# Results of seven experts by way of a table in device memory, in a two-layer decoder trunk

## The chip, the cores and the metric

The kernel runs on one core of a Trainium2 chip. The metric is the device time of one execution in microseconds (us), lower being better; where several runs are given, it is their median. A profiled execution gives a span (first to last instruction of the program) and a trace of every instruction and transfer.

The engines are called TensorE (PE in the rows), VectorE (DVE), ScalarE (ACT), GpSimd (POOL) and SyncE (SP). SBUF is the on-chip memory, PSUM the memory that TensorE's products go to (tile PS, eight banks of 128x512).

## What is computed

Two layers, each with three token mixers and a channel mixer, for 256 tokens of 1024 channels in float32. The second layer's channel mixer, the last thing before the output, picks two of eight experts per token:

```python
def swiglu(h, w1, w3, w2):
    return (jax.nn.silu(h @ w1) * (h @ w3)) @ w2

def moe_swiglu(h, w_router, w1, w3, w2):
    logits = (h @ w_router).astype(jnp.float32)
    top_val, top_idx = lax.top_k(logits, TOP_K)          # TOP_K = 2
    probs = jax.nn.softmax(top_val, axis=-1)
    combine = jnp.sum(jax.nn.one_hot(top_idx, N_EXPERTS, dtype=jnp.float32) * probs[..., None], axis=-2)
    out = jnp.zeros_like(h)
    for e in range(N_EXPERTS):                            # 8 experts, inner width 3584
        out = out + combine[..., e:e + 1] * swiglu(h, w1[e], w3[e], w2[e])
    return out
```

The layer's result is `x + moe_swiglu(h, ...)`. The mixers, norms and the dense channel mixer of the first layer are untouched by the change.

## The kernel before

**Arithmetic.** Every product of float32 matrices is made of three: each operand is split into a high part (hi, rounded to the format that TensorE multiplies fast) and a residue (lo), and `products` (lines 476 to 478) adds hi x hi, hi x lo and lo x hi in PSUM.

**Weight units.** SyncE loads weights in units of 1 MB, in a fixed order, into six slots `raw`. ScalarE copies each unit to one of three slots `hi` (line 1186); VectorE subtracts that copy from the raw unit, which gives `lo`, in the raw slot's own place (line 1681). Both call this step `prep`. TensorE counts a unit as used (`unit_used`) after its last product with it. The load of unit u waits for unit u-6 to be used, ScalarE's copy for unit u-3. Each engine works through its own list in order, so a `prep` stands between other operations at a place written out by hand.

**Experts.** There are 128 slots for the tokens of an expert. Per expert there are seven steps (`step`, inner width 512 each): `up` for w1 and w3 (four units, into PS banks 0 and 1), SiLU by ScalarE (f_s), the product by VectorE (f_g), four transposes (`turn_f`, line 1063), the split into fT_hi (ScalarE) and fT_lo (VectorE), and `down` for w2 (two units, summed in banks 4 and 5). Banks 4 and 5 hold the expert's result, one row per slot, after its last `down`, which TensorE runs inside the next expert's first step. If more than 128 tokens chose one expert, the flag `r_flag` starts a second round of all experts (`turn` 1) for the rest; in the measured data it doesn't run.

**Which tokens.** `r_t[:, 14]` holds for each token and expert the token's slot. VectorE makes the 0/1 matrix `pick` (token by slot, `choose`); `find_rows` multiplies it by token numbers, VectorE turns that into indices (`keep_row`), and GpSimd fetches the tokens' rows from `fn_dram` by an indirect transfer into `e_rows` (line 2455), half an expert ahead. `turn_rows` transposes them for the next expert.

**Adding results, before.** In the next expert ScalarE copies banks 4 and 5 to y_hi and VectorE makes y_lo (`results`). TensorE turns `pick` (two transposes, line 1099), ScalarE copies that to `pickT`, and `scatter` (line 1026) multiplies it by y_hi and y_lo: eight matmuls of 128x512 put each slot's row back at its token, in banks 4 to 7. VectorE adds that to `x` with the token's weight for the expert, `r_t[:, 15]` (`add_to_x`, line 2235, two operations). For the last expert `scatter_last` and `add_last` do it in halves, and SyncE stores `x`.

GpSimd has nothing else to do in the experts than the gathers of rows.

## Time and profile before

| | us |
|---|---|
| median of 3 runs | 2058.24 |
| lowest and highest run | 2054.41, 2058.87 |
| profiled execution | 2054.22 |
| its span | 2052.4 |

| engine | busy us | share of the span |
|---|---|---|
| TensorE (PE) | 2012.1 | 98% |
| VectorE (DVE) | 1580.0 | 77% |
| ScalarE (ACT) | 1247.0 | 61% |
| GpSimd (POOL) | 13.9 | 1% |

The experts take the second half, from about 1077 us on. Of the 516.53 MB that were moved, 336 units of 1 MB are expert weights, and in that half the rate is 329 to 382 GB/s per slice of the page, against 80 to 277 GB/s in the first half. A matmul's duration in the trace includes the time it takes to run through the array; matmuls overlap, so their pace is read from how far apart they start. Idle time of an engine that isn't the bottleneck costs nothing.

### The profile page before, as it was taken

Reading aid. Unit: us, or ns where it says so; the run is one execution under the profiler, and the core shown is the slowest. Engines: PE = TensorE matmul, PEld = TensorE weight load, DVE = VectorE, ACT = ScalarE, POOL = GpSimd, SP = SyncE. Lnnn points to the kernel's source line nnn. Section 1 sums busy time; section 2 is a strip of 40 time slices with the busy share of each in tenths; the row PEclk is TensorE's granted clock in tenths of the full one; section 3 lists DMA queues with packets and bytes.
Section 4 is the critical chain, followed back from the end, with each engine's and each line's share of the span. In section 5 each row is a group of like instructions: output and inputs, shape, how many; then the busy total and the mean of one; then the engine's idle time right before and its main releaser. Section 6 shows DMA issues by size and latency. Waiting matters only on the chain.

```text
span 2052.4 us, 28693 instructions
## 1 busy us (share of the span) xinstructions
PE 2012.1 (98%) x10737; PEld 1722.1 (84%) x10737; DVE 1580.0 (77%) x1218; ACT 1247.0 (61%) x1060; POOL 13.9 (1%) x21
## 2 busy tenths in 40 slices
PE   9999999999999999999989999999999999999998
PEld 8988888789998987888878888888888888888887
DVE  5778855755445878865768898888989889898987
ACT  5655455443334664455447777777777777777775
POOL 0000000000000000000000000000000000000000
PEclk9999999999999999999999999999999999999999
DMA  8523455255554523455249999999999999999996
GB/s 277 167 80 106 143 182 184 83 184 185 184 184 146 183 83 103 144 172 182 98 154 329 378 364 380 370 358 377 358 382 353 380 369 357 377 358 381 354 374 243
DMA packets 240765, 516.53 MB, mean 252 GB/s; under 512 B 11528, under 2 KB 34312, under 8 KB 240686
## 3 DMA queue, kind: packets, MB, share of 16 engines
q1 hardware_dynamic: 238274, 507.33, 69.9%
q0 software_dynamic: 2144, 7.88, 1.1%
q8 instruction: 55, 0.90, 0.2%
q10 hardware_dynamic: 268, 0.22, 0.0%
q14 instruction: 24, 0.20, 0.0%
HBM read 513.28 MB, written 2.12 MB: 251 GB/s over the span
## 4 chain that ended last, share of the span: by engine, by line
PE 92%; DVE 4%; issue 2%; ACT 2%; DVEq 0%; ACTq 0%
PE PS L476 27%; PE PS L478 27%; PE PS L477 27%; PE PS L560 7%; PE PS L1063 1%; ACT hi L1186 1%; PE PS L1026 1%; PE PS L780 1%; PE PS L694 0%; PE PS L811 0%; DVE t_n L1704 0%; PE PS L1014 0%; DVE b_gc L2014 0%; PE PS L493 0%; PE PS L649 0%
## 5 line engine op out<-in xcount | busy, mean ns | idle before, releaser
L1681 DVE TENSOR_TENSOR lo<-raw,hi 128x2048 fp32r<-128x2048 f32 x481 | 1095.8, 2290 | 289.9 <-ACT hi L1186 287.6
L1186 ACT ACTIVATE hi<-raw 128x2048 fp32r<-128x2048 f32 x481 | 919.7, 1915 | 314.1 <-PE PS L478 307.9
L476 PE MATMUL PS<-hi,e_hi 128*128 128x512 f32 x896 | 355.1, 396 | 1.4 <-DVE e_lo L1704 1.4
L478 PE MATMUL PS<-hi,e_lo 128*128 128x512 f32 x896 | 349.5, 390 | 0.0
L477 PE MATMUL PS<-lo,e_hi 128*128 128x512 f32 x896 | 349.0, 389 | 0.0
L476 PE MATMUL PS<-hi,actT_hi 128*128 128x512 f32 x640 | 253.4, 396 | 3.7 <-DVE lo L1681 3.1
L478 PE MATMUL PS<-hi,actT_lo 128*128 128x512 f32 x640 | 249.6, 390 | 0.0
L477 PE MATMUL PS<-lo,actT_hi 128*128 128x512 f32 x640 | 249.2, 389 | 0.0
L476 PE MATMUL PS<-hi,fT_hi 128*128 128x512 f32 x536 | 208.7, 389 | 0.0
L478 PE MATMUL PS<-hi,fT_lo 128*128 128x512 f32 x536 | 208.7, 389 | 0.0
L477 PE MATMUL PS<-lo,fT_hi 128*128 128x512 f32 x536 | 208.6, 389 | 0.0
L478 PEld LDWEIGHTS PS<-hi,e_lo 128*128 128x128 f32 x896 | 168.2, 188 | 36.1
L476 PEld LDWEIGHTS PS<-hi,e_hi 128*128 128x128 f32 x896 | 168.3, 188 | 34.6 <-DVE e_lo L1704 1.6
L477 PEld LDWEIGHTS PS<-lo,e_hi 128*128 128x128 f32 x896 | 168.5, 188 | 33.3
L476 PE MATMUL PS<-actT_hi,hi 128*128 128x256 f32 x672 | 191.4, 285 | 1.4 <-DVE actT_lo L1704 1.4
L478 PE MATMUL PS<-actT_hi,lo 128*128 128x256 f32 x672 | 190.7, 284 | 0.0
L477 PE MATMUL PS<-actT_lo,hi 128*128 128x256 f32 x672 | 190.7, 284 | 0.0
L476 PEld LDWEIGHTS PS<-hi,actT_hi 128*128 128x128 f32 x640 | 120.3, 188 | 28.2 <-ACT hi L1186 3.9
L478 PEld LDWEIGHTS PS<-hi,actT_lo 128*128 128x128 f32 x640 | 120.1, 188 | 25.4
L477 PEld LDWEIGHTS PS<-lo,actT_hi 128*128 128x128 f32 x640 | 120.3, 188 | 23.6
L476 PEld LDWEIGHTS PS<-actT_hi,hi 128*128 128x128 f32 x672 | 129.5, 193 | 2.3 <-issue 1.8
L477 PEld LDWEIGHTS PS<-actT_lo,hi 128*128 128x128 f32 x672 | 129.6, 193 | 0.4
(329 smaller groups left out, 2112.0 us busy)
## 6 DMA issues: line engine op xcount, KB each, us to landing
raw<-in_moe_w SPq DMA_DIRECT2D x336, 1024.0 KB, 5.3
raw<-in_w_in SPq DMA_DIRECT2D x92, 1024.0 KB, 5.1
raw<-in_ffn_w SPq DMA_DIRECT2D x33, 1024.0 KB, 5.2
raw<-in_w_br SPq DMA_DIRECT2D x12, 1024.0 KB, 5.0
raw<-in_w_out SPq DMA_DIRECT2D x8, 1024.0 KB, 5.1
bias<-hankel_dram POOLq DMA_DIRECT2D x1, 1536.0 KB, 12.7
x<-in_x SPq DMA_DIRECT2D x2, 512.0 KB, 5.5
f_gain<-in_norm_ffn POOLq DMA_DIRECT2D x2, 512.0 KB, 3.8
```

The source lines that it names most:

```text
L476: pe.matmul(out, a_hi, b_hi, start=first, stop=False, skip_group_check=True)
L477: pe.matmul(out, a_hi, b_lo, start=False, stop=False, skip_group_check=True)
L478: return pe.matmul(out, a_lo, b_hi, start=False, stop=last, skip_group_check=True)
L560: return pe.matmul(out, a, b, start=first, stop=last)
L780: ins = pe.transpose(PS[:, 4 + h // 2, ((h % 2) * TT + t) * P:((h % 2) * TT + t + 1) * P], c_n[:, t, hs(h)], ident)
L1026: ins = pe.matmul(PS[:, 4 + 2 * t + half, :], pickT[:, t, :], src[:, half * 512:(half + 1) * 512], start=part == 0, stop=part == 1)
L1063: ins = pe.transpose(PS[:, 2, j * P:(j + 1) * P], f_g[0][:, j * P:(j + 1) * P], ident)
L1186: act.activation(hi[prog.u % SPLIT][:, :], raw[slot][:, :], COPY).then_inc(hi_made.sem, 1)
L1681: dve.tensor_tensor(lo[prog.u % RAW][:, :], raw[prog.u % RAW][:, :], hi[s][:, :].bitcast(F32), ALU.subtract).then_inc(lo_made.sem, 1)
```

## The change

For `turn` 0, which is all that runs on the measured data, the first seven experts' results no longer pass through TensorE.

- ScalarE copies banks 4 and 5 to a float32 tile `y_out` (`results_out`) in the place of y_hi, at the same point of its list. GpSimd writes it to a table `y_dram` in device memory, 128 rows of 4 KB per expert (0.52 MB).
- The scatter, the transposes of `pick`, the copy to `pickT`, y_lo and `add_to_x` are gone in these experts. The last expert keeps `scatter_last` and `add_last`, with its own transposes.
- VectorE computes in the first expert, for each token and each of its two choices, the row of the table (`places`, seven small operations): the slot plus 128 times the expert's number. A token whose choice is the last expert (or lies past slot 128) gets a row of the table's last 128, which hold zeros; GpSimd writes these at the start.
- In the last expert GpSimd waits for the seventh write, starts four indirect transfers into `y_back` (two choices by two halves of the tokens, 0.52 MB each), multiplies each by the token's weight and adds it to `x`: eight operations on 128x1024 with both inputs in SBUF. `add_last` waits for them (`y_added`).

```diff
+        def results_out(n, used):
+            act.wait_ge(unit_used.sem, used)
+            act.wait_ge(fn_out.sem, n * 16 + 32)
+            act.activation(y_out[:, :], bank(4, 5), COPY).then_inc(y_hi_made.sem, 1)
...
             up(0)
-            if not first:
+            if turn and not first:
                 scatter(n - 1)
-            for t in range(TT):
-                ins = pe.transpose(PS[:, 3, t * P:(t + 1) * P], pick[:, t, :], ident)
-            ins.then_inc(pickT_done.sem, 1)
+            if turn or last:
+                for t in range(TT):
+                    ins = pe.transpose(PS[:, 3, t * P:(t + 1) * P], pick[:, t, :], ident)
+                ins.then_inc(pickT_done.sem, 1)
             up(1)
-            if not first:
-                pe.wait_ge(s_read.sem, s_read.count(2 * n - 1))
+            if turn and not first:
+                pe.wait_ge(s_read.sem, s_read.count((n - SPREAD) * 2 - 1))
+            elif not first:
+                pe.wait_ge(y_hi_made.sem, n)
             down(base, first=True)
...
         def add_last(n, e, turn):
+            dve.wait_ge(y_added.sem, 2 * TT)
...
+        def places():
+            dve.wait_ge(slots_here.sem, 6)
+            pos, base, val, part = (r_t[:, n, :] for n in (14, 16, 17, 18))
+            tt(val, pos, base, ALU.add).then_inc(dve_step.sem, 1)
+            dve.wait_ge(dve_step.sem, prog.step())
+            dve.scalar_tensor_tensor(val, pos, float(P), val, ALU.is_lt, ALU.mult).then_inc(dve_step.sem, 1)
+            dve.wait_ge(dve_step.sem, prog.step())
+            for k in range(2):
+                tt(part, r_t[:, 4 + k, :], val, ALU.mult).then_inc(dve_step.sem, 1)
+                dve.wait_ge(dve_step.sem, prog.step())
+                dve.tensor_reduce(r_t[:, 19, k * TT:(k + 1) * TT], part.rearrange("p (t e) -> p t e", t=TT),
+                                  AX.X, ALU.add).then_inc(dve_step.sem, 1)
+                dve.wait_ge(dve_step.sem, prog.step())
+            dve.tensor_scalar(y_at[:, :], r_t[:, 19, 0:2 * TT], float(SPREAD * P), None, ALU.add).then_inc(row_made.sem, 1)
...
             prep(2)
             multiply(base + 1, U + 8)
             prep(2)
+            if first and turn == 0:
+                places()
             if not last:
                 choose(n + 1, e + 1, turn)
             low(base + 1)
...
         for n in range(1, E):
-            pool.wait_ge(row_made.sem, n)
+            pool.wait_ge(row_made.sem, n + 1)
             if n > 1:
                 pool.wait_ge(e_done.sem, e_done.count(2 * n))
             pool.indirect_dma_start(e_rows[:, :], None, fn_dram[:, :],
                                     bass.IndirectOffsetOnAxis(ap=row_i[:, 0:1], axis=0)).then_inc(e_rows_here.sem, 16)
+            pool.wait_ge(y_hi_made.sem, n)
+            pool.dma_start(y_dram[(n - 1) * P:n * P, :], y_out[:, :]).then_inc(fn_out.sem, 16)
+        pool.wait_ge(fn_out.sem, 32 + 16 * SPREAD)
+        for c in range(2 * TT):
+            pool.indirect_dma_start(y_back[:, c, :], None, y_dram[:, :],
+                                    bass.IndirectOffsetOnAxis(ap=y_at[:, c:c + 1], axis=0)).then_inc(e_rows_here.sem, 16)
+        pool.wait_ge(e_rows_here.sem, 16 * (SPREAD + 2 * TT))
+        for c in range(2 * TT):
+            t = c % TT
+            pool.tensor_tensor(y_back[:, c, :], y_back[:, c, :], r_t[:, 11, c:c + 1].broadcast_to([P, D]), ALU.mult)\
+                .then_inc(y_scaled.sem, 1)
+            pool.wait_ge(y_scaled.sem, c + 1)
+            if c >= TT:
+                pool.wait_ge(y_added.sem, c - TT + 1)
+            pool.tensor_tensor(x[:, t, :], x[:, t, :], y_back[:, c, :], ALU.add).then_inc(y_added.sem, 1)
```

What this does to the lists. TensorE at the boundary from the first expert to the second, between the two halves of the second step's `up`, before (the numbers at the ends of names tell buffers apart):

```order
L478 MATMUL PS<-hi_61,e_lo_153 128x512
L1022 REGISTER_ALU
L1026 MATMUL PS<-y_hi,pickT 128x512
L1026 MATMUL PS<-y_lo,pickT 128x512
L1026 MATMUL PS<-y_hi,pickT 128x512
L1026 MATMUL PS<-y_lo,pickT 128x512
L1026 MATMUL PS<-y_hi,pickT 128x512
L1026 MATMUL PS<-y_lo,pickT 128x512
L1026 MATMUL PS<-y_hi,pickT 128x512
L1026 MATMUL PS<-y_lo,pickT 128x512
L1099 MATMUL PS<-consts,pick 128x128 x2
L476 MATMUL PS<-hi_62,e_hi_151 128x512
```

and now:

```order
L485 MATMUL PS<-hi_61,e_lo_153 128x512
L489 REGISTER_ALU
L483 MATMUL PS<-hi_62,e_hi_151 128x512
L484 MATMUL PS<-lo_56,e_hi_151 128x512
L485 MATMUL PS<-hi_62,e_lo_153 128x512
```

The eight matmuls of the scatter and the two transposes are gone, and the products of the next half of `up` follow those of the first.

VectorE in the first expert, second step, now, with the seven operations of `places` between two residues (`lo`), the pick and fT_lo:

```order
L1699 TENSOR_TENSOR lo_55<-raw_49,hi_61 128x2048
L1722 TENSOR_TENSOR r_t<-r_t 128x16
L2277 SCALAR_TENSOR_TENSOR r_t<-r_t 128x16
L1722 TENSOR_TENSOR r_t<-r_t 128x16
L2282 TENSOR_REDUCE r_t<-r_t 128x2
L1722 TENSOR_TENSOR r_t<-r_t 128x16
L2282 TENSOR_REDUCE r_t<-r_t 128x2
L2285 TENSOR_SCALAR y_at<-r_t 128x4
L2234 TENSOR_SCALAR pick<-slots,r_t 128x128 x2
L1722 TENSOR_TENSOR fT_lo_139<-PS,fT_hi_137 128x512
L1699 TENSOR_TENSOR lo_56<-raw_50,hi_62 128x2048
```

Before, the pick followed the residue `lo_55` at once.

GpSimd's list from the last gather of rows to its end, now:

```order
L2501 DMA e_rows<-fn_dram,row_i 128x1024
L2504 DMA y_dram<-y_out 128x1024
L2507 DMA y_back<-y_dram,y_at 128x1024 x4
L2512 TENSOR_TENSOR y_back<-y_back,r_t 128x1024
L2517 TENSOR_TENSOR x<-x,y_back 128x1024
L2512 TENSOR_TENSOR y_back<-y_back,r_t 128x1024
L2517 TENSOR_TENSOR x<-x,y_back 128x1024
L2512 TENSOR_TENSOR y_back<-y_back,r_t 128x1024
L2517 TENSOR_TENSOR x<-x,y_back 128x1024
L2512 TENSOR_TENSOR y_back<-y_back,r_t 128x1024
L2517 TENSOR_TENSOR x<-x,y_back 128x1024
```

Before, its list ended with the seventh gather of rows; the write of a result now follows each of the seven.

## Rows read from the trace of the kernel before

**Rows 1.** Busy time per engine in a stretch of the experts, with its heading.

```profile
core 0: us, PE busy (x) PEld busy (x) DVE busy (x) ACT busy (x) POOL busy (x), PEclk, DMA share, GB/s
1320.00:1440.00 120.00, 120.00 (x551) 99.46 (x550) 107.28 (x65) 88.39 (x60) 0.95 (x1) 1.00 1.00 368
```

**Rows 2.** Waits from 1065 us on: who for whom, us in total, times, longest.

```profile
ACT hi L1186 <- PE PS L478: 137.5, 213, 3.9
...
PE PS L476 <- DVE e_lo L1704: 1.4, 1, 1.4
```

**Rows 3.** Order in time, last expert: start us, us, engine, line, tiles, idle before.

```profile
1965.17 1.92 ACT L1186 ACTIVATE hi<-raw 128x2048 fp32r<-128x2048 f32 x1 [0.80 <-PE PS L478]
1967.89 1.92 ACT L1186 ACTIVATE hi<-raw 128x2048 fp32r<-128x2048 f32 x1 [0.80 <-PE PS L478]
...
1967.26 2.28 DVE L1681 TENSOR_TENSOR lo<-raw,hi 128x2048 fp32r<-128x2048 f32 x1
```

**Rows 4.** Groups from 1050 us on: busy us, mean ns of one, idle before.

```profile
L1681 DVE TENSOR_TENSOR lo<-raw,hi 128x2048 fp32r<-128x2048 f32 x336 | 764.8, 2289 | 105.5 <-ACT hi L1186 104.7
...
L1704 DVE TENSOR_TENSOR f_g<-f_s,PS 128x512 f32<-128x512 f32 x56 | 38.1, 680 | 0.1
...
L2235 DVE SCALAR_TENSOR_TENSOR x<-PS,r_t,x 128x1024 f32<-128x1024 f32 x14 | 17.3, 1276 | 0.0
...
L1704 DVE TENSOR_TENSOR y_lo<-PS,y_hi 128x1024 fp32r<-128x1024 f32 x7 | 8.5, 1218 | 0.0
```

**Rows 5.** Tile raw (1200 to 2040 us); transfers (1371 to 1378 us); one stretch; issues.

```profile
L1681 DVE TENSOR_TENSOR lo<-raw,hi x292: 2277/2292/2295, 1200.1 to 2038.0; 128x2048 fp32r<-128x2048 f32 x146
...
DMA to landing us min/median/max: 4.8/5.3/7.9
...
q0 software_dynamic: 144, 0.52, 19.6%
...
1380.00:1390.00 10.00, 10.00 (x48) 8.26 (x47) 8.86 (x5) 7.51 (x6) 0.00 (x0) 1.00 1.04 399
...
raw<-in_moe_w SPq DMA_DIRECT2D x336, 1024.0 KB, 5.3
```

**Rows 6.** TensorE in time at the last boundary.

```profile
1940.36 0.40 PE L478 MATMUL PS<-hi,e_lo 128*128 128x512 f32 x1
1940.59 0.40 PE L1026 MATMUL PS<-y_hi,pickT 128*128 128x512 f32 x1
...
1942.46 0.38 PE L1099 MATMUL PS<-consts,pick 128*128 128x128 f32 x2
1942.59 0.47 PE L476 MATMUL PS<-hi,e_hi 128*128 128x512 f32 x1
1942.91 0.39 PE L477 MATMUL PS<-lo,e_hi 128*128 128x512 f32 x1
```

**Rows 7.** VectorE in time at the same boundary.

```profile
1938.22 4.50 DVE L1681 TENSOR_TENSOR lo<-raw,hi 128x2048 fp32r<-128x2048 f32 x2
```

**Rows 8.** VectorE in time: small operations of the routing, a residue of the first expert.

```profile
1063.99 0.17 DVE L2372 SCALAR_TENSOR_TENSOR r_t<-r_t 128x16 f32<-128x16 f32 x1
1064.20 0.17 DVE L2361 TENSOR_REDUCE r_t<-r_t 128x2 f32<-128x16 f32 x1
...
1109.12 4.59 DVE L1681 TENSOR_TENSOR lo<-raw,hi 128x2048 fp32r<-128x2048 f32 x2 [0.30 <-ACT hi L1186]
```

**Rows 9.** GpSimd in time.

```profile
1059.78 0.39 POOL L2443 CAST slots<-slots_i 128x256 f32<-128x256 int32 x1
...
1060.43 0.18 POOL L2447 CAST ids<-slots_i 128x2 f32<-128x2 int32 x1
...
1129.11 2.70 POOL L2455 DMA_INDIRECT e_rows<-fn_dram,row_i  x1 [60.99 <-DVE row_i L2221]
1249.64 0.96 POOL L2455 DMA_INDIRECT e_rows<-fn_dram,row_i  x1 [117.83 <-DVE row_i L2221]
1370.72 0.95 POOL L2455 DMA_INDIRECT e_rows<-fn_dram,row_i  x1 [120.12 <-DVE row_i L2221]
```

More of the change, by code:

```diff
@@ L68 @@
 PAIRS = E // 2
+SPREAD = E - 1
 K_ID, K_LE, K_GT, K_M0, K_MT, K_N = 0, 1, 2, 3, 4, 11
@@ L1019, in scatter @@
         def scatter(n):
-            pe.wait_ge(pickT_made.sem, n + 1)
-            pe.wait_ge(y_lo_made.sem, y_lo_made.count(n + 1))
+            pe.wait_ge(pickT_made.sem, n - SPREAD + 1)
+            pe.wait_ge(y_lo_made.sem, y_lo_made.count(n - SPREAD + 1))
             for t in range(TT):
@@ L1030, in scatter_last @@
         def scatter_last(n, turn):
-            pe.wait_ge(pickT_made.sem, n + 1)
+            pe.wait_ge(pickT_made.sem, n - SPREAD + 1)
             for half in range(2):
                 if half:
-                    pe.wait_ge(y_lo_made.sem, y_lo_made.count(n + 1))
+                    pe.wait_ge(y_lo_made.sem, y_lo_made.count(n - SPREAD + 1))
                 else:
@@ L1113, in expert @@
             if not last:
-                if not first:
-                    pe.wait_ge(s_read.sem, s_read.count(2 * n))
+                if turn and not first:
+                    pe.wait_ge(s_read.sem, s_read.count((n - SPREAD) * 2))
                 if turn == 0:
@@ L1133, in experts @@
             if turn:
-                pe.wait_ge(s_read.sem, s_read.count(2 * E * turn))
+                pe.wait_ge(s_read.sem, s_read.count(2))
             n = E * turn
@@ L1599, in expert @@
             prep(2 if first else 4)
-            if not first:
+            if not first and turn:
                 results(U + 4)
+            elif not first:
+                results_out(n - 1, U + 4)
             high(base)
@@ L1606, in expert @@
             prep(1)
-            act.wait_ge(pickT_done.sem, pickT_done.count(n + 1))
-            act.activation(flat(pickT), PS[:, 3, 0:T], COPY).then_inc(pickT_made.sem, 1)
+            if turn or last:
+                act.wait_ge(pickT_done.sem, pickT_done.count(n - SPREAD + 1))
+                act.activation(flat(pickT), PS[:, 3, 0:T], COPY).then_inc(pickT_made.sem, 1)
             prep(3)
@@ L2211, in choose @@
             dve.wait_ge(e_done.sem, e_done.count(2 * n))
-            dve.wait_ge(pickT_done.sem, pickT_done.count(n))
+            if turn:
+                dve.wait_ge(pickT_done.sem, pickT_done.count(n - SPREAD))
             for t in range(TT):
@@ L2278, in expert @@
             prep(1 if first else 2)
-            if not first:
+            if turn and not first:
                 results(n - 1)
@@ L2283, in expert @@
             prep(1)
-            if not first:
+            if turn and not first:
                 for t in range(TT):
@@ L2409, in moe @@
                 prep(3)
-                dve.wait_ge(s_read.sem, s_read.count(2 * E))
+                dve.wait_ge(s_read.sem, s_read.count(2))
                 experts(1)
@@ L2447, in _ @@
         pool.tensor_copy(ids[:, :], slots_i[:, 0:TT]).then_inc(slots_here.sem, 1)
+        pool.wait_ge(slots_here.sem, 4)
+        pool.iota(slots_i[:, 0:TT * E], pattern=[[0, TT], [P, E]], base=-SPREAD * P, channel_multiplier=0)\
+            .then_inc(slots_here.sem, 1)
+        pool.wait_ge(slots_here.sem, 5)
+        pool.tensor_copy(r_t[:, 16, :], slots_i[:, 0:TT * E]).then_inc(slots_here.sem, 1)
+        pool.memset(y_out[:, :], 0.0).then_inc(slots_here.sem, 1)
         pool.wait_ge(norm_made.sem, norm_made.at(1, 5))
@@ L2577, in store @@
             load(out[:, :, 0:512], x[:, :, 0:512], out_here)
-            sp.wait_ge(s_read.sem, s_read.count(2 * E * (turn + 1)))
+            sp.wait_ge(s_read.sem, s_read.count(2 + 2 * E * turn))
             load(out[:, :, 512:D], x[:, :, 512:D], out_here)
```

13 lines of the change are left out of this document (10 added, 3 removed).

## Prediction, made before the changed kernel was run

> **What bounds the kernel now.** I read the profile in this order: the busy time by stretch, the waits, the order in time at an expert's boundary, then the transfers. From about 1077 us to 2043 us the eight experts run. TensorE is busy for all 120.00 us of a 120 us stretch there, at a granted clock of 1.00, and VectorE for 107.28 us [rows 1]. TensorE waits for nothing in that stage beyond the start: ScalarE and VectorE wait for it [rows 2]. So a microsecond taken from TensorE's list there is a microsecond of the span, as long as the feeders keep up. The feeders are close behind, and the change loads one of them. Three margins matter.
>
> *Pace.* TensorE uses up one weight unit (1 MB of raw weights) each 2.72 us: two copies by ScalarE that each waited for TensorE start that far apart [rows 3]. With the four transposes a step of six units takes 16.80 us, so 2.80 us per unit on average.
>
> *VectorE.* The copy of unit u starts when unit u-3 is used up, and TensorE wants unit u two units, 5.44 us, after that: 1965.17 + 5.44 = 1970.61. The residue (lo) is made at 1967.26 + 2.28 = 1969.54 [rows 3]. The margin is 1.07 us. Free time is 2.80 - 2.29 (one residue) - (0.68 + 0.68)/6 = 0.28 us per unit [rows 4]; the row of f_g stands for fT_lo too, which is of the same size.
>
> *Transfers.* A unit's load starts when the unit six before it is used up, and ScalarE wants it three units, 8.16 us, later. Loads land after 5.3 us in the median and 7.9 us at most [rows 5]. Six units in 16.80 us are 374 GB/s, and when a 0.52 MB gather has come between, the engines move 399 GB/s with a share of 1.04 [rows 5]: I take 400 GB/s as what they can do. Little is left.
>
> **The change part by part.**
>
> *TensorE loses the scatter.* At a boundary the first scatter matmul starts at 1940.59 and the next product of the expert at 1942.59; the product before it started 0.23 us earlier, an ordinary spacing [rows 6]. So 2.00 us go: 1.87 us for eight matmuls (1940.59 to 1942.46) and 0.13 us for the two transposes; the first product after them also holds 0.09 us more than the ordinary spacing (0.32 for 0.23 us) [rows 6]. 2.09 x 7 = 14.6 us. (Seven scatters go, and seven pairs of transposes; the last boundary keeps its pair and the first expert loses one, which is the same count.) Is the next unit ready 2 us earlier? Its residue is the first of two that start at 1938.22 and take 4.50 us together [rows 7], so it is done at 1940.47, 0.12 us before TensorE now asks for it. It just fits; if not, a tenth or two per boundary goes back.
>
> *VectorE loses* per boundary the residue of the result, 1.22 us, and two additions of 1.28 us [rows 4]. VectorE isn't the bound, so that is worth nothing by itself; it holds the 0.12 us above.
>
> *ScalarE* writes the same copy of the result to another tile and drops the copy of the turned matrix: nothing. It and TensorE now wait for that copy and for the write of an expert ago; both were done long before (more than ten microseconds of products lie between).
>
> *VectorE gets seven small operations* in the first expert that compute the places. Such operations start 0.21 us apart [rows 8]: 1.5 us. Behind them in VectorE's queue stand the pick, fT_lo and the residue that starts at 1109.12. Before it are 0.30 us of idle [rows 8]; its margin is about the 1.07 us above, less what pick costs. So TensorE waits some 0.5 us, once (0 to 1.5).
>
> *GpSimd's seven writes of results*, 0.52 MB each, go beside the loads like the gather of rows, which costs TensorE nothing now, although loads then take up to 7.9 us to land [rows 2, 5]. One more such burst per expert stands under the 8.16 us: nothing, by 0.26 us. The zeroing and its write come before the first expert, off the chain.
>
> *Four gathers at once, in the last expert.* 4 x 0.52 MB, with the last write of 0.52 MB just ahead, are 2.6 MB; at 0.399 MB per us they hold the loads back by 6.6 us. Then a load lands after 5.3 + 6.6 = 11.9 us, against 8.16 + 1.07 = 9.2 us: TensorE waits 2.7 us. The low end is 0 (the loads go first). At the high end each gather adds what the single one does at most, 7.9 - 5.3 = 2.6 us: 5.3 + 10.4 - 9.2 = 6.5 us.
>
> *Eight GpSimd operations on 128x1024*, with two inputs in SBUF each, in the last expert. My estimate is that they begin some 20 us after the last expert's boundary at 1940 us (copy, write, gathers of 5 to 12 us each step) and end within 40 us more; add_last needs them only after the last product, 100 us after that boundary. So their own time is hidden by some 40 us of products. What isn't hidden is what they do to VectorE. GpSimd has no such operation in the trace. The nearest rows are its casts with one input: 0.39 us for 256 columns and 0.18 us for 2, so 0.82 ns a column and 1.02 us for 1024 [rows 9]. With two inputs read one behind the other it is 0.18 + 2 x 0.84 = 1.86 us, which I take; the low bound is 1.02 us, the high one 2.70 us, GpSimd's longest instruction [rows 9]. If they leave VectorE alone they cost nothing. If a residue (two inputs in SBUF) can't start while one of them runs, the two take turns: a pair takes p + 2.29 us where a unit may take 2.80 us, so VectorE falls back p - 0.51 us each time, eight times, less 1.4 us (two of them fall beside operations that read PSUM) and less the margin of 1.1 us. For p = 1.86 us: 8 x 1.35 - 2.5 = 8.3 us. For 1.02 us it is 1.6 us, for 2.70 us 15.0 us. The only GpSimd work beside a residue in the trace is a gather's issue, and no residue of the 292 took over 2.295 us [rows 5]; but an issue is no arithmetic, and that row decides nothing.
>
> The Trainium skill (SBUF — State Buffer, section "Who interferes with whom") says that a VectorE instruction with two SBUF inputs and a GpSimd instruction that reads SBUF exclude each other for the whole instruction. No row here shows or denies it. By that rule the hold is real, and the sum keeps its 8.3 us; without it the sum would be 8.3 us lower. The Trainium skill (GPSIMD Engine Reference, section "Elementwise — side-by-side cycle accounting") gives 4497 ns for a two-input add of 2048 columns; an estimate from it is 2.25 us for 1024, and by that page the hold would be 11.4 us and the kernel level with before. It gives 2293 ns for VectorE, and the trace agrees with 2289 ns.
>
> *Sum*, against the profiled execution (span 2052.4 us, time 2054.2 us, 4.0 us under the median of the three runs): -14.6 + 0.5 + 2.7 + 8.3 = -3.1 us, so 2051.1 us for it and 2058.24 - 3.1 = 2055.1 us for the median.
>
> **The rivals.** About 0.2%, 4.1 us, is what a measurement of this kernel can tell from no change.
>
> 1. *Hold* (the forecast): GpSimd's operations and VectorE's residues take turns. For it: both read two tiles in SBUF, and VectorE is 89% busy with 1.07 us of margin, so anything that holds it shows. 2055.1 us; 2048 to 2062 us over the bounds of p.
> 2. *No hold*: 2055.1 - 8.3 = 2046.8 us, and 2044 us if the gathers cost nothing either. For it: nothing in the trace shows the two engines in each other's way.
> 3. *Long GpSimd operations, the slower side*: the same turns with p well above its bound. Its first gather took 2.70 us where the next took 0.96 us [rows 9], so its instructions can be long. With p = 3.0 us the hold is 8 x 2.49 - 2.5 = 17.4 us, and the kernel takes 2064 us. It is slower by over 0.2% once p is above 2.8 us.
> 4. *The scatter's time isn't given back*: VectorE's residue, 0.12 us ahead now, comes late at every boundary and TensorE waits for it as long as it multiplied before. Half of the gain lost would make 2055.1 + 7.3 = 2062.4 us. Against it: VectorE drops 3.8 us of work at the same place.
>
> **How the numbers follow.** Hold 60%, no hold 25%, long operations 10%, gain lost 5%. The likeliest gives 2055 us. The range takes in no hold with free gathers, 2044 us, and hold up to its high bound, 2062 us; it leaves out most of rivals 3 and 4. Faster by over 0.2% means under 2054.1 us: all of no hold, and that part of hold in which p is under about 1.7 us or the gathers are cheap, 25 points: 0.50. Slower means over 2062.4 us: rival 3 and a part of rival 4, 0.12. The rest, 0.38, is within 0.2%. Hold's own range is 2048 to 2062 us.
>
> **What the profile after would show.** The spacing of experts, 121.1 us from one gather of rows to the next [rows 9], falls to 119.0 us with no wait of TensorE; if it doesn't, rival 4. In the last expert TensorE waits, first for ScalarE's copy while the gathers are under way (2.7 us), then for VectorE's residue, in pieces of up to 2 us, while GpSimd's eight operations run (8.3 us); residues start when a GpSimd operation ends. If VectorE's residues keep their pace there, it is no hold, and the forecast is 8 us too high. GpSimd's mean duration tells 1.86 us from 2.25 or 3.0 us. A wait of TensorE at 1109 us tells the price of the places. What would make all of it wrong is loads that come late in every expert because of the added write, whose margin is 0.26 us.

## Result: 0.85% slower, and where the time went

| | us, median (lowest to highest) | ratio to before, 95% interval |
|---|---|---|
| before | 2057.4 (2054.4 to 2058.9) | |
| changed | 2074.7 (2072.1 to 2078.1) | 1.0085 [1.0068, 1.0103] |

The profiled execution of the changed kernel took 2078.1 us, its span 2076.1 us, 23.7 us more than the span before. Of these 1.7 us lie ahead of the first gather of rows, 9.7 us between that gather and the last one, and 12.3 us from there to the end. One execution of a later run (e8) took 2182.6 us at a granted clock of 0.87 over the whole run and is left out of its median.

**The experts.** GpSimd in time, changed kernel (start us, us, engine, line, operation, idle before it), the gathers of rows and the writes of results:

```profile
1249.99 0.98 POOL L2501 DMA_INDIRECT e_rows<-fn_dram,row_i  x1 [37.43 <-DVE row_i L2240]
1331.23 0.56 POOL L2504 DMA_DIRECT2D y_dram<-y_out  x1 [80.26 <-ACT y_out L1590]
1369.22 0.99 POOL L2501 DMA_INDIRECT e_rows<-fn_dram,row_i  x1 [37.44 <-DVE row_i L2240]
1460.46 0.56 POOL L2504 DMA_DIRECT2D y_dram<-y_out  x1 [90.25 <-ACT y_out L1590]
1498.44 0.99 POOL L2501 DMA_INDIRECT e_rows<-fn_dram,row_i  x1 [37.43 <-DVE row_i L2240]
```

From 1249.99 to 1369.22 an expert takes 119.2 us, against 121.1 us before [rows 9]: the scatter's time is given back. The next one takes 129.2 us, and so does one more (1617.68 to 1747.16 us, 129.5 us). Those two are the starts of experts 3 and 5, where the loop over pairs of experts jumps back to its head.

**The two stops.** TensorE's waits, whole span, changed kernel (us in total, times, longest):

```profile
PE PS L483 <- issue: 15.1, 4, 7.3
PE PS L483 <- DVE lo L1699: 15.1, 13, 2.1
```

The first row, in which TensorE waits for nothing that the profile shows, was almost nothing before:

```profile
PE PS L476 <- issue: 0.6, 2, 0.3
```

Two of its four waits now, 14.6 us together, lie behind 1065 us, in the experts, where there was none before. In order of time at the first of the two places:

```profile
1432.05 0.60 PE L1069 MATMUL PS<-consts,f_g 128*128 128x128 f32 x4
...
1435.11 2.29 DVE L1699 TENSOR_TENSOR lo<-raw,hi 128x2048 fp32r<-128x2048 f32 x1 [0.74 <-ACT hi L1195]
...
1439.99 0.76 PE L483 MATMUL PS<-hi,e_hi 128*128 128x512 f32 x1 [7.34 <-issue]
1440.13 0.33 PEld L484 LDWEIGHTS PS<-lo,e_hi 128*128 128x128 f32 x1
1440.56 0.63 PE L484 MATMUL PS<-lo,e_hi 128*128 128x512 f32 x1
```

The last residue was done at 1437.40 us, everybody had stopped by then, and TensorE still stood until 1439.99 us. After that its matmuls start 0.43 us apart in place of 0.23 us. Busy time per engine in the stretches around it (us, count; then the granted clock, the DMA share, GB/s):

```profile
1428.00:1436.00 8.00, 4.65 (x23) 3.65 (x21) 6.95 (x6) 5.05 (x4) 0.00 (x0) 0.93 1.03 365
1436.00:1444.00 8.00, 4.01 (x10) 3.17 (x11) 1.41 (x1) 0.00 (x0) 0.00 (x0) 0.50 0.18 71
1444.00:1452.00 8.00, 8.00 (x34) 6.58 (x33) 3.58 (x2) 5.43 (x4) 0.00 (x0) 0.93 0.64 223
```

The granted clock of 0.50 is the lower of the two levels, 1.2 GHz; it had begun to fall while TensorE stood (0.73 from 1434 to 1436 us). So a stop costs 7.3 us of standing and about 3 us of slow running: 129.2 - 119.2 = 10.0 us, and 10.2 us the second time. One more line of the page has changed, the queue that fetches TensorE's code (packets, MB, share): before it was 55 packets and 0.90 MB, now

```profile
q8 instruction: 73, 1.20, 0.2%
```

that is 16 KB a packet, 18 packets more. They lie in the expert loop's second and third turns: nine from 1431.9 to 1665.6 us and nine from 1681.2 to 1913.6 us, where the kernel before has no packet between 1380.1 and 1931.3 us. (The stretch from 1400 to 1900 us, which is used below, holds no line for this queue before and 18 packets now; one of these, at 1416.6 us, still belongs to the first turn, and the last of the nine lies behind 1900 us.) One packet is in the 2 us around TensorE's stop (1430 to 1432 us) and the next in 1437 to 1439 us, just before it goes on.

**The last expert.** From the last gather of rows to the end of the span the kernel before takes 197.4 us and the changed one 209.7 us, although a scatter of 2 us is gone there too. GpSimd's eight operations and VectorE beside them, changed kernel:

```profile
1989.22 3.95 POOL L2512 TENSOR_TENSOR y_back<-y_back,r_t 128x1024 f32<-128x1024 f32 x1
1993.25 4.33 POOL L2517 TENSOR_TENSOR x<-x,y_back 128x1024 f32<-128x1024 f32 x1
1997.54 3.95 POOL L2512 TENSOR_TENSOR y_back<-y_back,r_t 128x1024 f32<-128x1024 f32 x1
2001.57 4.33 POOL L2517 TENSOR_TENSOR x<-x,y_back 128x1024 f32<-128x1024 f32 x1
```

```profile
1991.94 16.10 DVE L1699 TENSOR_TENSOR lo<-raw,hi 128x2048 fp32r<-128x2048 f32 x4
2007.96 0.68 DVE L1722 TENSOR_TENSOR f_g<-f_s,PS 128x512 f32<-128x512 f32 x1
2008.56 4.48 DVE L1699 TENSOR_TENSOR lo<-raw,hi 128x2048 fp32r<-128x2048 f32 x2
```

Four residues take 16.10 us while GpSimd works, 4.0 us each, and two take 4.48 us, 2.24 us each, when it has ended. GpSimd's operations start one per residue. The waits of 1930 to 2076 us show both prices that the prediction had named:

```profile
PE PS L483 <- DVE lo L1699: 11.7, 10, 2.1
...
ACT hi L1195 <- DMA raw<-in_moe_w: 10.1, 9, 3.1
```

### The profile page after: what moved, and what is told of

It is laid out like the page before. It is cut to its first block, busy times and chain, and to the rows that moved or that the text cites. A ratio compares the mean times of both kernels' runs of the same rounds, so it can differ in the third digit from the quotient of the medians.

```text
span 2076.1 us, 28514 instructions
## 1 busy us (share of the span) xinstructions
PE 2009.6 (97%) x10667; PEld 1714.9 (83%) x10667; DVE 1570.9 (76%) x1204; ACT 1246.1 (60%) x1053; POOL 59.7 (3%) x44
## 4 chain that ended last, share of the span: by engine, by line
PE 88%; DVE 6%; issue 3%; ACT 2%; DMA 1%; ACTq 0%; DVEq 0%; SPq 0%
PE PS L483 26%; PE PS L485 26%; PE PS L484 26%; PE PS L567 7%; DVE lo L1699 2%; ACT hi L1195 1%; PE PS L1069 1%; DMA raw<-in_moe_w 1%; PE PS L787 1%; PE PS L701 0%; PE PS L818 0%; DVE t_n L1722 0%; PE PS L1020 0%; DVE b_gc L2032 0%; PE PS L656 0%
## 5 line engine op out<-in xcount | busy, mean ns | idle before, releaser
L1699 DVE TENSOR_TENSOR lo<-raw,hi 128x2048 fp32r<-128x2048 f32 x481 | 1109.0, 2318 | 322.0 <-ACT hi L1195 320.2
L483 PE MATMUL PS<-hi,e_hi 128*128 128x512 f32 x896 | 357.6, 399 | 23.3 <-issue 14.6
L485 PE MATMUL PS<-hi,fT_lo 128*128 128x512 f32 x536 | 208.7, 389 | 0.0
L484 PE MATMUL PS<-lo,fT_hi 128*128 128x512 f32 x536 | 208.7, 389 | 0.0
L484 PEld LDWEIGHTS PS<-lo,actT_hi 128*128 128x128 f32 x640 | 120.3, 188 | 23.5
```

The costliest lines, as they stand in the source:

```text
L483: pe.matmul(out, a_hi, b_hi, start=first, stop=False, skip_group_check=True)
L484: pe.matmul(out, a_hi, b_lo, start=False, stop=False, skip_group_check=True)
L485: return pe.matmul(out, a_lo, b_hi, start=False, stop=last, skip_group_check=True)
L1699: dve.tensor_tensor(lo[prog.u % RAW][:, :], raw[prog.u % RAW][:, :], hi[s][:, :].bitcast(F32), ALU.subtract).then_inc(lo_made.sem, 1)
```

## How the runs are compared

Kernels that are the same up to the experts, but for a warm-up matmul or a few waits, reach them at different times, 1077.0 to 1081.9 us in the traces (the kernel before is the earliest), and the times of one kernel lie up to 6.7 us apart (e2). That the one makes the other is likely, but only one execution of each kernel has a trace. The experts themselves repeat to a few tenths, but for single late loads (see e8). So beside the medians I use two stretches of each trace: from the first gather of rows to the last, 6 experts, and from the last one to the end of the span.

| kernel | first to last gather, us | last gather to end, us | median, us | ratio, 95% interval |
|---|---|---|---|---|
| before | 725.9 | 197.4 | | |
| changed | 735.6 | 209.7 | 2074.7 | 1.0085 [1.0068, 1.0103] |
| e1: before, 21 warm-ups | 743.7 | 197.6 | 2073.1 | 1.0079 [1.0062, 1.0096] |
| e2: changed, 23 warm-ups | 715.2 | 208.7 | 2057.3 | 1.0006 [0.9996, 1.0016] |
| e3: e2, gathers only | 715.4 | 199.5 | 2049.6 | 0.9962 [0.9948, 0.9976] |
| e4: e2, writes only | 715.2 | 195.5 | 2043.0 | 0.9939 [0.9922, 0.9955] |
| e5: e3, VectorE adds | 715.3 | 200.6 | 2048.7 | 0.9965 [0.9951, 0.9979] |
| e6: e5, gathers paced | 715.9 | 197.7 | 2048.0 | 0.9953 [0.9936, 0.9969] |
| e7: before, 30 warm-ups | 725.9 | 197.1 | 2059.5 | 1.0014 [1.0005, 1.0024] |
| e8: changed, 31 warm-ups | 716.4 | 208.7 | 2061.6 | 1.0023 [1.0013, 1.0033] |
| e9: before, 400 waits | 729.9 | 197.8 | 2083.0 | 1.0131 [1.0108, 1.0153] |
| e10: changed, 8 waits | 715.2 | 208.1 | 2058.5 | 1.0012 [1.0001, 1.0022] |
| e11: e3, one-input copies | 715.2 | 202.3 | 2050.5 | 0.9971 [0.9960, 0.9983] |
| e12: e2, all paced | 715.2 | 202.2 | 2051.0 | 0.9975 [0.9965, 0.9984] |

The kernel before had a median of 2057.1 us in the runs beside e1 to e4, 2055.4 us beside e5 to e8 and 2056.4 us beside e9 to e12.

## The two stops: where the loop lies in TensorE's code

My theory after the result: TensorE holds a limited number of 16 KB blocks of its code. An instruction is 64 bytes in the compiled program, so a block is 256 of them. Counted there, without labels, the loop over pairs of experts begins at TensorE's instruction 10,947 before and at 10,943 in the changed kernel; it is 1764 instructions long before and 1720 now. The head has moved because the first expert, which stands ahead of the loop, has lost its two transposes. If a block edge lies between the two, the old loop covers seven blocks and the new, shorter one eight. The rival: the added writes, or the new waits for them, stop TensorE.

Each 128x128 warm-up matmul at the program's start is four instructions, so their number moves the loop and touches nothing near it.

```diff
 # e1, kernel before
-        for _ in range(22):
+        for _ in range(21):
             mm(PS[:, 7, 0:P], ones, ones)
```

> The kernel before with 21 instead of 22 matmuls in the first warm-up run at the program's start, nothing else: the matmul is four TensorE instructions, so everything behind it stands four instructions earlier in TensorE's code, as it does in the changed kernel. Theory A (instruction blocks: the two TensorE stops of 7.3 us at the starts of experts 3 and 5 are fetches of code, because the expert loop's head now lies just ahead of a block boundary and the loop covers one block more): the two stops of 7 to 8 us appear at the starts of experts 3 and 5, each followed by a stretch at granted clock 0.50, 10 us each, so 2057.4 + 20 = 2077 us (2074 to 2081), and the instruction queue moves about 73 packets in place of 55. Theory B (the stops come from the added writes and their waits): no stop, 2057.4 us, 0.1 us less for the matmul.

Measured: 2073.1 us, ratio 1.0079. Experts of 130.4 and 129.5 us at the same two places, 121.1 us elsewhere, and 73 packets (the other queue of instructions keeps its 24, so q8 is TensorE's). TensorE in time, e1, at the first of them:

```profile
1437.62 0.60 PE L1063 MATMUL PS<-consts,f_g 128*128 128x128 f32 x4
1444.57 0.76 PE L476 MATMUL PS<-hi,e_hi 128*128 128x512 f32 x1 [6.35 <-issue]
1445.13 0.63 PE L477 MATMUL PS<-lo,e_hi 128*128 128x512 f32 x1
```

The kernel before, with nothing of the change in it, loses 17.8 us in its experts by the removal of one warm-up matmul.

```diff
 # e2, changed kernel
-        for _ in range(22):
+        for _ in range(23):
             mm(PS[:, 7, 0:P], ones, ones)
```

> The changed kernel with 23 instead of 22 matmuls in the first warm-up run: TensorE's expert loop stands where it stood before the change. Theory A (instruction blocks): both stops are gone, 2074.7 - 20.2 = 2054.5 us (2052 to 2058), all gathers of rows are 119 to 119.5 us apart, and the queue of instruction fetches is back at about 55 packets. Theory B (the added writes cause the stops): 2074.7 us, stops as in the changed kernel.

Measured: 2057.3 us, ratio 1.0006, no stop, 55 packets. Its first and last gather (duration ns, start us of the first and of the last of the seven):

```profile
L2501 POOL DMA_INDIRECT e_rows<-fn_dram,row_i x7: 978/984/1024, 1129.5 to 1844.7; - x7
```

(1844.7 - 1129.5) / 6 = 119.2 us each. The writes are all there, so they are not the cause.

Two more moved the loop further, to tell how the place matters.

```diff
 # e7, kernel before                      # e8, changed kernel
-        for _ in range(22):              -        for _ in range(22):
+        for _ in range(30):              +        for _ in range(31):
```

> The kernel before with 30 instead of 22 warm-up matmuls (32 TensorE instructions more ahead of the expert loop; the matmuls run while loads arrive). The loop's head then lies 32 instructions inside its block instead of next to the edge, but its last instructions pass the edge at the other end, so it covers eight blocks where it covered seven. Theory A (the loop must cover no more than seven blocks): both stops come back, 2057.1 + 16 = 2073 us, and the instruction queue moves over 70 packets. Rival C (what counts is where the head lies, just ahead of an edge or not): no stop, 2057 to 2058 us.

Measured: no stop, 55 packets, 725.9 us for six experts as before. Theory A as I had put it is wrong here: only the loop's last four instructions lie in the eighth block (a few more if labels count), and that costs nothing. The median is 2059.5 us, and the experts begin later (1082.7 us in the trace, outside the 1077.0 to 1081.9 us above): the added matmuls don't seem to be free at the start.

> The changed kernel with 31 instead of 22 warm-up matmuls (36 TensorE instructions more): its loop is 44 instructions shorter than the one before, so at the same place of the head it still ends inside the seventh block. Theory A and rival C both: no stops, 2057 to 2058 us, 55 packets of instructions. Theory D (only the exact place of before is free of stops, or more warm-up matmuls cost time themselves): over 2060 us.

Measured: no stop, 55 packets, 716.4 us. The median of 2061.6 us, over 2060, is what I had listed for theory D, but by its second half only: the first product of the experts is at 1084.2 us, against 1077.5 us in e2 (up to 4.9 us of that can be the spread above). The six experts take 1.2 us more than in e2, 1.0 us of it in one wait: at 1391.8 us, behind a gather of rows, the load of a unit is late, and TensorE's next product starts 1.20 us after the one before in place of 0.23 us.

So was it the number of blocks, or a head just ahead of an edge (rival C)? e9 puts the head well inside a block, 56 instructions ahead of its end, and the loop's end well inside the eighth; e10 repeats e2 without touching the matmuls.

```diff
 # e9, kernel before (range(400)); e10, changed kernel (range(8))
         pe.wait_ge(tiny_made.sem, 5)
+        for _ in range(400):
+            pe.wait_ge(tiny_made.sem, 5)
         for _ in range(22):
```

> The kernel before with 400 waits that are met at once ahead of the first warm-up matmul: 200 TensorE instructions more in the code, no matmul more. The expert loop then begins in the middle of a block of 256 instructions and ends in the middle of the eighth block (0.79 to 7.68 blocks from the edge). Theory A in its new form (eight blocks stay and the next is fetched ahead, so what counts is that the block behind the loop's last is asked for too): both stops come back, the experts last 941 us from the first gather of rows to the end in place of 923, over 70 packets of instructions. Rival C (only a head that lies just ahead of an edge stops TensorE): 923 us and 55 packets. The 200 instructions themselves cost some us at the program's start, ahead of the experts.

> The changed kernel with its 22 warm-up matmuls and eight waits that are met at once ahead of them, which are four TensorE instructions: the loop lies where it lay before the change, by another route than the matmul. Theory A and rival C: no stops, 924 us from the first gather of rows to the end, 2056 to 2058 us. If the number of warm-up matmuls mattered in itself: stops as in the changed kernel, 2074 us.

Measured, e10: no stop, 55 packets, 715.2 us, 2058.5 us. The place counts, not the matmuls. Measured, e9: the fetches are back, 74 packets on the page and in the stretch from 1400 to 1900 us

```profile
q8 instruction: 18, 0.29, 0.2%
```

as in the changed kernel, and TensorE stops at both jumps, but for 1.9 us, not for 7: the experts take 927.7 us from the first gather to the end, between the 923 and the 941 expected. TensorE in time, e9:

```profile
1460.11 0.60 PE L1065 MATMUL PS<-consts,f_g 128*128 128x128 f32 x4
1462.33 0.47 PE L476 MATMUL PS<-hi,e_hi 128*128 128x512 f32 x1 [1.63 <-DVE lo L1683]
1462.64 0.40 PE L477 MATMUL PS<-lo,e_hi 128*128 128x512 f32 x1
```

(The row names VectorE, whose residue ends at 1461.82 us here. In the kernel before TensorE goes on at 1433.90 us at this place, ahead of the end of the same residue, so it isn't what TensorE wants.) The clock stays at 1.00 from 1458 to 1464 us, and the expert takes 122.9 us in place of 121.1 us. Most of what is more in the 2083.0 us are the 400 waits at the start: the first matmul comes at 23.5 us in place of 1.8 us.

| kernel | head and end of the loop, in blocks from the edge | code packets, 1400 to 1900 us | stop |
|---|---|---|---|
| before | 0.00 to 6.89 | 0 | none |
| e7 | 0.13 to 7.02 | 0 | none |
| e8 | 0.13 to 6.84 | 0 | none |
| e2, e10 | 0.00 to 6.72 | 1 | none |
| e9 | 0.78 to 7.67 | 18 | 1.9 us |
| e1 | -0.02 to 6.88 | 18 | 6.6 and 6.9 us |
| changed | -0.02 to 6.70 | 18 | 7.6 and 7.5 us |

(The edge is taken at instruction 10,947; the stop is the distance of TensorE's starts across the jump, in the kernel before under 0.1 us. The one packet of e2 and e10 is the first turn's last.) Two things together fit all rows; that they are the mechanism is inferred. First, whether the loop is fetched again in every turn: it isn't while the loop's blocks and the one fetched ahead of need are eight or fewer. Before: seven and one. e7: eight, and its eighth is entered for a few instructions only, and no packet comes after the first turn. e1 and changed: eight, whose last is run nearly to its end, so a ninth would be fetched, and the oldest, with the head, goes; nine packets in each of the later turns are what that gives. Second, how long it stops: with 56 instructions left in the head's block (e9) one block must come in, and its fetch began at the end of the turn, in 1458 to 1461 us; with at most four instructions left in the head's block (e1, changed), the next block is missing too and is fetched after it. In the changed kernel the packets start at 1431.9 and 1437.7 us, and at the second stop at 1681.2 and 1685.8 us, 5.8 and 4.6 us apart, and TensorE goes on 2.3 and 2.5 us after the start of the second. In e9 they lie as far apart, 5.4 us, in 1458 to 1461 and in 1464 to 1466 us, but there TensorE has work from the first. The first point rests on eight kernels and on the packets; that fetches follow one another some 5 us apart because the one waits for the other is read from their times alone. No run shows whether the full load on the transfers (365 GB/s) makes them slow.

The Trainium skill (Runtime: NRT & Kernel Launch, section "Instruction fetch mechanics") gives TensorE 2048 instructions of instruction memory, filled in blocks of 256 in order while the current one runs, and warns that a taken branch to a block that isn't held stops the engine for a fetch. The runs agree: 2048 is eight blocks. A note in the same section, which reckons with 32 KiB, says that only two blocks are held and that a branch beyond them waits for a fetch. For TensorE that doesn't hold here: a loop over seven blocks jumped back twice, and its second and third turns had not one fetch.

## The last expert: GpSimd's operations and the gathers

Both kernels leave out work, on top of e2, so that each part's price shows.

```diff
 # e3: no operations of GpSimd
         def add_last(n, e, turn):
-            dve.wait_ge(y_added.sem, 2 * TT)
...
-        for c in range(2 * TT):
-            t = c % TT
-            pool.tensor_tensor(y_back[:, c, :], y_back[:, c, :], ...)
...
-            pool.tensor_tensor(x[:, t, :], x[:, t, :], y_back[:, c, :], ALU.add).then_inc(y_added.sem, 1)
 # e4: no gathers of results either
-        for c in range(2 * TT):
-            pool.indirect_dma_start(y_back[:, c, :], None, y_dram[:, :], ...)
```

> The changed kernel with 23 warm-up matmuls, without GpSimd's eight operations and without the wait for them ahead of the last expert's additions; the contributions of the first seven experts are left out of the output. Theory H (hold: GpSimd's operations and VectorE's residues take turns, pairs 4.15 us apart where 2.80 us is the pace): 8 to 11 us less than the kernel with 23 warm-ups, so 2045 us (2043 to 2047), and no residue spacing of 4 us in the last expert. Theory N (the last expert is late because the four gathers hold back the loads of weights, and the operations only fall on that): 0 to 2 us less, so 2053 us.

Measured: 2049.6 us, 7.7 us less than e2 by the medians; 9.2 us less in the last stretch (208.7 to 199.5 us). Residues take 2290 ns in the mean again. That is theory H, though the median lies above its 2043 to 2047 us: e2, from which it was reckoned, took 2057.3 and not 2054.5 us, and by the medians alone the 7.7 us lie just under its 8 to 11.

> The kernel with 23 warm-up matmuls and without GpSimd's eight operations, now also without the four gathers of results; the first seven experts' contributions are left out of the output, their results are still written to the table. Theory H (the gathers are cheap, 2.7 us by my sum, 3 to 4 us by the waits of the changed kernel's trace): 2057.4 - 14.6 + 0.5 = 2043 us (2041 to 2045). Theory N (the gathers are what makes the last expert late): 8 to 11 us under the kernel with the gathers. If the scatter's 2.09 us per expert were not given back in full, it would be over 2045 us here, where nothing else of the change is left.

Measured: 2043.0 us, as theory H has it. But its price for the gathers was too low: 4.0 us in the last stretch (6.6 us by the medians) against 2.7 us. Transfers from 1925 to 1960 us, e3 (count, size, median us from issue to landing):

```profile
q0 software_dynamic: 720, 2.62, 18.6%
...
raw<-in_moe_w SPq DMA_DIRECT2D x11, 1024.0 KB, 11.4
```

and e4, where only the write is left beside the loads:

```profile
raw<-in_moe_w SPq DMA_DIRECT2D x12, 1024.0 KB, 7.0
```

The slowest load of e3 in the last expert took 13.0 us, where I had 11.9 us.

**Do one-input operations hold VectorE too?** e11 puts sixteen copies of a fetched tile onto itself in the place of the eight operations, and leaves the addition out.

```diff
 # e11, on e2
+        for c in range(8 * TT):
+            pool.tensor_copy(y_back[:, c // 4, :], y_back[:, c // 4, :]).then_inc(y_added.sem, 1)
+            pool.wait_ge(y_added.sem, c + 1)
```

> The changed kernel with 23 warm-up matmuls, GpSimd's eight two-input operations replaced by sixteen copies of a fetched 128x1024 tile onto itself, one input each; the first seven experts' contributions are left out of the output. By the casts before, one should take 1.02 us. If one-input operations hold VectorE's residues too, each pair takes 3.3 us against 2.80 us: 16 x 0.51 - 1.1 = 7 us over the kernel with the gathers alone, 2056.5 us. If only two-input operations of GpSimd exclude a residue: 0 to 1 us over it, 2049.6 to 2050.5 us, and residues keep their pace.

Measured: 2.8 us over e3 in the last stretch (0.9 us by the medians), so neither. GpSimd and VectorE in time, e11:

```profile
1948.54 2.15 POOL L2511 COPY y_back<-y_back 128x1024 f32<-128x1024 f32 x2 [6.93 <-DMA y_back<-y_dram,y_at]
```

```profile
1965.53 11.65 DVE L1699 TENSOR_TENSOR lo<-raw,hi 128x2048 fp32r<-128x2048 f32 x4
```

Two copies with VectorE all but idle take 2.15 us, 1.04 us each, the 1.02 us that the casts gave. Beside residues, copies and residues go one to one at 3.05 us a pair, as the starts of single residues show; the four in the row above average 2.91 us, since the first of them is shorter. So copies hold a residue as well, for 0.8 us each, but that is only a little over VectorE's free time of 2.80 - 2.29 us: 16 x (3.05 - 2.80) = 4 us less the margin of 1.1 us is 2.9 us, and 2.8 us were measured. My 3.3 us for the pair, the full sum, was too much.

**Can VectorE's free time pay for GpSimd's operations?** e12 starts one gather per step (`pool.wait_ge(f_silu.sem, ...)`, ScalarE's SiLU of the step), and runs that gather's two operations as soon as it has landed.

```diff
 # e12, on e2
         for c in range(2 * TT):
+            pool.wait_ge(e_rows_here.sem, 16 * (SPREAD + c))
+            pool.wait_ge(f_silu.sem, STEPS_DENSE + STEPS_EXPERT * SPREAD + 2 + c)
             pool.indirect_dma_start(y_back[:, c, :], None, y_dram[:, :], ...)
+            pool.wait_ge(e_rows_here.sem, 16 * (SPREAD + c + 1))
+            pool.tensor_tensor(y_back[:, c, :], ...)
+            pool.tensor_tensor(x[:, t, :], x[:, t, :], y_back[:, c, :], ALU.add)
```

> The changed kernel with 23 warm-up matmuls, but one gather per step of the last expert, and that gather's two GpSimd operations right behind its landing. Per step VectorE loses 2 x 1.35 us by turns and has 1.1 to 1.7 us free, so it falls back 1.0 to 1.6 us per step, 4 to 6.4 us in all less the margin of 1.1 us: 3 to 5.3 us, with 1 us for the paced gathers. The last expert's stretch (from the last gather of rows to the end) then takes 200 to 202 us in place of 208.7, and the kernel 2049.5 to 2051.5 us. If free time between the operations were of no use to VectorE, the hold would stay at 8 to 9 us: 2053 to 2054 us.

Measured: 202.2 us for the last stretch, 2051.0 us. The same work costs 6.5 us less only because it is spread; by e6 below some 3 us of that are the gathers' and the rest is the operations'. GpSimd and VectorE in time, e12, the fourth of the four. The residue starts while the first of GpSimd's two operations runs and takes 3.64 us in place of 2.29 us:

```profile
2000.36 1.89 POOL L2513 TENSOR_TENSOR y_back<-y_back,r_t 128x1024 f32<-128x1024 f32 x1 [7.10 <-DMA y_back<-y_dram,y_at]
2002.33 4.33 POOL L2518 TENSOR_TENSOR x<-x,y_back 128x1024 f32<-128x1024 f32 x1
```

```profile
2000.75 3.64 DVE L1699 TENSOR_TENSOR lo<-raw,hi 128x2048 fp32r<-128x2048 f32 x1 [0.35 <-ACT hi L1195]
```

1.89 us is the shortest of all the two-input operations in these traces; the 1.86 us of the prediction was a good bound.

## A version that beats both kernels

VectorE has 1.7 us free per step of six units, and one fused operation weighs and adds in one pass what GpSimd does in two.

```diff
 # e5, on e3 (DVE, last expert, behind steps 3 to 6; gathers start together)
+        def add_back(c):
+            dve.wait_ge(e_rows_here.sem, 16 * (SPREAD + 2 * TT))
...
+            dve.scalar_tensor_tensor(x[:, t, :], y_back[:, c, :], r_t[:, 11, c:c + 1], x[:, t, :],
+                                     ALU.mult, ALU.add).then_inc(y_added.sem, 1)
 # e6: as e5, add_back(c) waits for 16 * (SPREAD + c + 1), and GpSimd's list has
+            pool.wait_ge(e_rows_here.sem, 16 * (SPREAD + c))
+            pool.wait_ge(f_silu.sem, STEPS_DENSE + STEPS_EXPERT * SPREAD + 2 + c)
             pool.indirect_dma_start(y_back[:, c, :], None, y_dram[:, :], ...)
```

> The changed kernel with 23 warm-up matmuls, GpSimd's eight operations replaced by four fused ones of VectorE (fetched rows times the token's weight, plus x, 128x1024), one behind the third, fourth, fifth and sixth step of the last expert; the four gathers start together as before. VectorE has 2.80 - 2.29 - 0.23 = 0.28 us per unit free, 1.7 us per step, and one such operation should take 1.2 to 1.3 us. If VectorE has room for them: 0 to 1.5 us over the kernel with the gathers alone (2049.6), so 2050.5 us. If the cost lay in the adding itself, wherever it is done, it stays near 2057 us.

Measured: 2048.7 us; the last stretch is 1.1 us over e3. The adding costs 1.1 us on VectorE and 9.2 us on GpSimd.

> The same, and GpSimd starts one gather per step of the last expert, each when ScalarE has made that step's SiLU, in place of four together. If the gathers' 6.6 us are loads queued behind a burst of 2 MB, one gather of 0.52 MB per step costs what a gather of rows costs, nothing to 1.5 us in all, and the kernel takes 2044 us (2042.5 to 2046.5). If 2 MB more cost what they cost however they are spread (2 MB at 0.38 to 0.40 MB per us are 5.2 us, since the engines carry no more than that), it stays at 2049 to 2050.5 us.

Measured: the last stretch is 197.7 us, 3.0 us under e5, with 0.4 us of waits of TensorE for VectorE left in it. By the medians (2048.0 against 2048.7 us) the two can't be told apart, so 2044 us was too low for a median, and the gain from pacing rests on the stretch alone. VectorE in time, e6:

```profile
2000.49 2.29 DVE L1699 TENSOR_TENSOR lo<-raw,hi 128x2048 fp32r<-128x2048 f32 x1
2002.70 1.28 DVE L2277 SCALAR_TENSOR_TENSOR x<-y_back,r_t,x 128x1024 f32<-128x1024 f32 x1
2003.90 6.69 DVE L1699 TENSOR_TENSOR lo<-raw,hi 128x2048 fp32r<-128x2048 f32 x3
```

Residues stay at 2.2 to 2.3 us. e6 computes all of the result, takes 0.9953 [0.9936, 0.9969] of the time before and is 1.3% faster than the change as made.

## Why the prediction was wrong, point by point

I forecast 2055.1 us, 2044 to 2062; it took 2074.7 us. Without the two stops (e2) it is 2057.3 us.

- **What failed: the count of the parts.** The sum held what the change does to the lists of work, and took TensorE's code itself to be free. Its place in memory was no term, and no rival named it. It was worth 735.6 - 715.2 = 20.4 us in the experts of the changed kernel (17.4 us by the medians), over five times the forecast gain of 3.1 us. The prediction did count that the first expert loses its transposes, for their 0.13 us; that everything behind them moves up by four instructions it left out.
- **Scatter, -14.6 us: mechanism right, a tenth too large: -13.4 us.** Set e4 beside before, each timed from its first product of the experts (1079.5 and 1077.0 us): e4 is 0.25 us ahead where the first expert has lost its transposes, 0.34 us behind after the places, and 12.8 us ahead behind the seventh boundary. So a boundary gives 1.9 us, not 2.09, and -13.4 + 0.6 (places) = -12.8 us. (The two stretches of the table show -12.6 us, the places included.) Where I wrote that the next residue just fits and that a tenth or two may go back, it did: in e4 TensorE's first product of that unit comes 0.38 us after the one before it (1574.38 to 1574.77 us), 0.15 us more than the ordinary 0.23.
- **Places, +0.5 us: right, 0.6 us.** In e2 0.73 us lie between the starts of two products at 1112 us, 0.5 us more than ordinary.
- **Gathers, +2.7 us (0 to 6.5): 4.0 us by the stretch, 6.6 us by the medians.** The slowest load took 13.0 us (e3), not 5.3 + 6.6 = 11.9 us. The part that was too small is the 5.3 us, which are the landing before the change: with the scatter gone, but no gathers of results, loads land in 6.3 us in the median (e4, 1200 to 1900 us). 6.3 + 6.6 - 9.2 = 3.7 us comes close to the 4.0 us; that is a sum made afterwards, and no run tests it.
- **Hold, +8.3 us: right, 9.2 us** (7.7 us by the medians). GpSimd's operations start 4.03 us (behind a multiplication) and 4.28 us (behind an addition) apart, 4.15 us in the mean, which is p + 2.29 with p = 1.86. All four parts: -13.4 + 0.6 + 4.0 + 9.2 = +0.4 us, and that is what the traces give from the first product of the experts to the end (975.4 us before, 975.8 us in e2). e2's ratio of 1.0006 [0.9996, 1.0016] is +1.2 us and holds it. So without the stops the kernel would have come out level, inside the forecast range; the sum of -3.1 us was 3.5 us too low, by 1.2 us in the scatter, 1.3 in the gathers, 0.9 in the hold and 0.1 in the places.
- **Rivals.** No hold is out (e3 against e2), so are operations with p of 3 us. The scatter's time is given back but for 0.2 us per boundary. "Loads late in every expert because of the added write" didn't happen: 119.2 us in each in e2. Loads did get closer to their margin (6.3 us in the median of e4), and once, in e8, one was late and cost 1.0 us.
- The forecast took hold, which is also what the Trainium skill says (SBUF — State Buffer, "Who interferes with whom"): the runs agree, with the 4.0 us per pair against 2.24 us for a residue alone. The one-input copies of e11 are a limit to that: a pair took 3.05 us, less than the full sum of 3.33 us. Its other figure (GPSIMD Engine Reference, "Elementwise — side-by-side cycle accounting", 2.25 us for 1024 columns as an estimate) is above the 1.89 us measured.

## What to carry to other kernels

Taking instructions out of a program moves all code behind them, and a hot loop that just fits into what the engine holds of its code can stop fitting: look at the packets of the instruction queue before and after, and at stops where a loop jumps back, before explaining the time by the work. Such a stop may stand as "issue" (the changed kernel, e1) or under the name of an engine that happened to end late (e9). GpSimd beside a VectorE that has little time free isn't a second pair of hands: each of its operations on 128x1024 took 0.8 us (one input) to 1.9 us (two inputs) of VectorE's time here, and the same sums cost 9.2 us on GpSimd and 1.1 us as one fused operation each on VectorE. Work that must share an engine or the transfers with a tight pipeline should come in pieces no larger than what is free in a step.

## What the runs showed of the hardware

- TensorE's code comes in packets of 16 KB. Loops of 1720 and 1764 instructions ran their second and third turns without a fetch at two places in the code each, and at two others all of it was fetched again in each turn, nine packets, at 8.4 to 10.3 us (head four instructions ahead of an edge) or 1.9 us (head 56 instructions ahead of one) per jump.
- After standing from 1432.7 to 1440.0 us TensorE ran at the lower level for some 5 us (granted clock 0.50 from 1436 to 1444 us); after standing for 1.9 us it kept 1.00.
- A one-input copy of 1024 columns on GpSimd takes 1.04 us alone and 2.98 us beside residues, at 3.05 us a pair, which is less than the sum of both alone (3.33 us).
